# The first attention layer's values made for all head pairs at once, before the first pair

## The reference

```
parts = h @ even_w_in           # 3 query groups | keys | values, 1024 columns each | 256 cross queries
k, v  = 16 heads of 64 each
for (window, dilation) in ((128, 1), (512, 4), (2048, 16)):      # three branches, each with its own queries
    scores = q_branch . k * 64**-0.5 + relative bias, masked     # p = exp(scores - max)
mix = (sum over branches of p @ v) / (sum over branches of row sums)    # one maximum for all three
x = x + concat(mix, cross attention) @ w_out
```

## Time and profile before

| | |
|---|---|
| profiled execution, its own time | 1534.58 us |
| its span, first to last instruction | 1532.8 us |
| around the span | 1.8 us |
| TensorE busy | 1513.6 us (99%), 8132 matmuls |
| VectorE, ScalarE, GpSimd busy | 1316.3 us (86%), 1124.7 us (73%), 95.3 us (6%) |
| mean granted TensorE clock | 0.996 of 2.4 GHz |
| first layer's attention, pair 0's first projection to the end of pair 7's mix | 37.96 to 200.90 us |

### The profile page before, as it was taken

The page is one execution under the profiler, slowest core; times in us unless marked ns, Lnnn a source line. Parts: engine busy times, 40 slices in busy tenths (PEclk is TensorE's granted clock), DMA queues, the critical chain, the costliest instruction groups (busy, mean ns, idle before and its releaser), DMA issues.

```text
span 1532.8 us, 25011 instructions
## 1 busy us (share of the span) xinstructions
PE 1513.6 (99%) x8132; PEld 1280.9 (84%) x8132; DVE 1316.3 (86%) x1783; ACT 1124.7 (73%) x1487; POOL 95.3 (6%) x70
## 2 busy tenths in 40 slices
PE   9999999999999999999999999999999999999997
PEld 8999978888898788888888888888888888888886
DVE  5788868777778879998998998998998998998997
ACT  6565566544557668788788888788788888878875
POOL 2422100000030000000000000000000000000000
PEclk9999999999999989999999999999999999999999
DMA  9944546666633579999999999999999999999992
GB/s 283 241 138 137 152 129 190 190 186 192 170 90 90 164 291 369 391 380 390 381 369 389 378 374 385 380 377 376 382 396 360 384 395 358 387 391 352 401 385 112
DMA packets 225973, 455.39 MB, mean 297 GB/s; under 512 B 12848, under 2 KB 119488, under 8 KB 225920
## 3 DMA queue, kind: packets, MB, share of 16 engines
q1 hardware_dynamic: 221712, 439.52, 79.5%
q0 software_dynamic: 4208, 15.22, 3.9%
HBM read 445.52 MB, written 9.18 MB: 297 GB/s over the span
## 4 chain that ended last, share of the span: by engine, by line
PE 93%; DVE 4%; ACT 1%; issue 1%; DMA 0%; SPq 0%; ACTq 0%; DVEq 0%
PE ps L815 26%; PE ps L817 26%; PE ps L816 26%; PE ps L1139 5%; PE ps L1141 3%; PE ps L1327 2%; PE ps L931 2%; PE ps L967 1%; PE ps L947 1%; DVE w_lo L1824 1%; PE ps L1269 0%; DMA big<-in_w_mem_kv 0%; DVE X L2030 0%; DVE small L1920 0%; DVE pr L2190 0%
## 5 line engine op out<-in xcount | busy, mean ns | idle before, releaser
L1824 DVE TENSOR_TENSOR w_lo<-big,w_hi 128x1024 fp32r<-128x1024 f32 (+1 forms) x830 | 977.6, 1217 | 121.4 <-ACT w_hi L1711 52.2
L1711 ACT CAST w_hi<-big 128x1024 fp32r<-128x1024 f32 x672 | 693.5, 1056 | 139.1 <-PE ps L817 135.5
L815 PE MATMUL ps<-w_hi,m_hi 128*128 128x512 f32 (+1 forms) x1008 | 392.6, 389 | 1.5 <-DVE w_lo L1824 1.3
L817 PE MATMUL ps<-w_hi,m_lo 128*128 128x512 f32 (+1 forms) x1008 | 389.7, 387 | 0.0
L816 PE MATMUL ps<-w_lo,m_hi 128*128 128x512 f32 (+1 forms) x1008 | 389.6, 386 | 0.0
L815 PEld LDWEIGHTS ps<-w_hi,m_hi 128*128 128x128 f32 x1008 | 189.5, 188 | 41.5 <-issue 4.3
L817 PEld LDWEIGHTS ps<-w_hi,m_lo 128*128 128x128 f32 x1008 | 189.5, 188 | 38.2
L816 PEld LDWEIGHTS ps<-w_lo,m_hi 128*128 128x128 f32 x1008 | 189.6, 188 | 36.9
L1364 ACT CAST w_hi<-big 128x1024 fp32r<-128x1024 f32 (+2 forms) x166 | 164.8, 1003 | 39.5 <-PE ps L817 32.4
L815 PE MATMUL ps<-w_hi,h_two 128*128 128x512 f32 (+1 forms) x464 | 182.1, 392 | 0.0
L817 PE MATMUL ps<-w_hi,h_two 128*128 128x512 f32 (+1 forms) x464 | 179.5, 387 | 0.0
(11 more groups left out here) (309 smaller groups left out, 1560.6 us busy)
## 6 DMA issues: line engine op xcount, KB each, us to landing
big<-in_odd_w_gate SPq DMA_DIRECT2D x112, 1024.0 KB, 7.3
big<-in_odd_w_up SPq DMA_DIRECT2D x112, 1024.0 KB, 7.7
big<-in_odd_w_down SPq DMA_DIRECT2D x112, 1024.0 KB, 7.6
big<-in_even_w_in SPq DMA_DIRECT2D x42, 512.0 KB, 4.3
big<-in_even_w_gate SPq DMA_DIRECT2D x22, 512.0 KB, 4.6
big<-in_even_w_up SPq DMA_DIRECT2D x22, 512.0 KB, 3.9
big<-in_even_w_down SPq DMA_DIRECT2D x22, 512.0 KB, 4.7
big<-in_w_out SPq DMA_DIRECT2D x20, 512.0 KB, 3.7
```

Of the source, the lines that this page charges most:

```text
L815: mm(dst, a[0], b[0], start=start, stop=False, **kw)
L817: return mm(dst, a[1], b[0], start=False, stop=stop, **kw)
L1711: nc.scalar.copy(w_hi[:, slot, :], ring[s][:, (u % 2) * UNIT:(u % 2 + 1) * UNIT]).then_inc(s_hi, 1)
L1824: return V.tensor_tensor(dst, src, lead.bitcast(F32), ALU.subtract)
```

## The change

The values of all eight pairs are made before pair 0, as 256 tokens x 1024 channels with tokens as rows. The activations are the stationary side and a weight unit of one contraction chunk and 1024 columns the moving side: 12 matmuls of 512 columns for each of eight units (`values_unit`). The results lie in banks 3, 4, 2 and 7, are copied to `XH` by four copies (`values_out`), and `mix` reads them there. A step has four projections instead of five, no transposes of values and no copies of them. The slots change: eight values units stand in the list after the memory's, in slots 2, 3, 4, 5, 0, 1, 2, 3, and the pairs use slots 0 to 3. The orders of TensorE, ScalarE and VectorE in a step are changed, TensorE's steps 0 to 3 are written out too, and the wait of a pair's first projection for `third_read` moves to its second.

```
@@ Units
+        for c in range(DC):
+            add(("values", c), (c + 2) % SLOTS)
         for g in range(PAIRS):
-            for m in range(NBR + 2):
+            for m in range(NBR + 1):
                 add(("pair", 0, g, m), m)
@@ banks of the values
-        def value_bank(pair):
-            return ps[:, 5 if pair.l == 0 else 2, 0:SEQ]
+        def value_bank(t, hf):
+            return ps[:, ((3, 4), (2, 7))[t][hf], :]
@@ SyncE, stream_loads
+                for c in range(DC):
+                    load(0, 0, [U.at[("values", c)]], w_in[0][:, c:c + 1, (NBR + 1) * D:(NBR + 2) * D])
@@ TensorE, project
-                if m == 0 and norm is None:
-                    pe.wait_ge(S["third_read"], PAIRS if pair.cross else pair.g)
+                if pair.cross:
+                    pe.wait_ge(S["third_read"], PAIRS)
+                elif m == 1 and pair.g > 0:
+                    pe.wait_ge(S["third_read"], pair.g)
@@ TensorE: turn_values goes, values_unit comes
+            def values_unit(c):
+                w = split(0, 0, [U.at[("values", c)]], 1)
+                pe.wait_ge(s_nlo, DC * NORM_MIX0 + c + 1)
                 for t in range(TT):
-                    last = tr(value_bank(pair)[:, tok(t)], vT[:, tok(t)], ident)
-                last.then_inc(S["turned_v"], 1)
+                    if c == 0:
+                        pe.wait_ge(s_me, 2 * t + 2)
+                    for hf in range(2):
+                        last = mm3(value_bank(t, hf), part(HS, A_, c, tok(t)), part(w, A_, 0, slice(hf * 512, (hf + 1) * 512)),
+                                   c == 0, c == DC - 1, skip_group_check=True)
+                        if c == DC - 1 and (t, hf) != (1, 1):
+                            last.then_inc(s_vmade, 1)
+                last.then_inc(s_used, 1)
@@ TensorE, mix
-                    v = vN[:, :, :]
+                    v = XH[:, :, pair.g * P:(pair.g + 1) * P]
@@ TensorE, step and stream
-                p(0)
-                turn_values(now)
-                p(1)
+                p(0, 1, 2)
                 turn_probs(now, 0)
-                p(2, 3)
+                p(3)
                 turn_probs(now, 1)
                 scores(nxt)
-                p(4)
                 mix(now)
+                for c in range(DC):
+                    values_unit(c)
                 for m in range(first.mats):
-                    project(first, m, norm if m == 0 else None)
-                pe.wait_ge(s_me, 2 * 2)
+                    if m < 2:
+                        pe.wait_ge(s_vout, m + 1)
+                    project(first, m)
+                pe.wait_ge(s_vout, 2 * TT)
                 scores(first)
-                steps(pe, step)
+                for g in range(NPAIR):
+                    step(pair_at(0, g), *(pair_at(0, h) if h < NPAIR else None for h in (g + 1, g + 2)))
@@ ScalarE, step (even pairs)
                     e(0)
-                    values()
                     h(0)
+                    exps(now, 1)
                     e(1)
-                    exps(now, 1)
                     h(1)
+                    e(2)
                     probsT(now, 0)
-                    e(2)
                     h(2)
                     e(3)
                     probsT(now, 1)
                     h(3)
-                    e(4)
                     h(4)
@@ ScalarE, stream
-            for m in range(3):
-                hi_mat(pair_at(0, 0), m)
+            for c in range(2):
+                hi(0, 0, [U.at[("values", c)]])
             mem_out(1)
             act.wait_ge(s_scrw, 16)
...
+                for c in range(2, DC):
+                    hi(0, 0, [U.at[("values", c)]])
+                for m in range(3):
                     hi_mat(a, m)
+                for t in range(TT):
+                    for hf in range(2):
+                        values_out(t, hf)
+                hi_mat(a, 3)
@@ VectorE, step (even pairs)
                     low(0)
-                    if isinstance(now.g, int) and now.g == LATE:
-                        head_probs(now, 1)
-                        low(1)
-                    else:
-                        low(1)
-                        head_probs(now, 1)
+                    head_probs(now, 1)
+                    low(1)
                     low(2)
-                    low(3)
...
                 if nxt is not None and not now.cross:
                     head_scores(nxt)
                 if now.kind == "even":
+                    low(3)
                     low(4)
```

More of the change, by code:

```diff
@@ L250, in __init__ @@
         self.kind = "cross" if self.cross else ("even", "odd")[l]
-        self.mats = 1 if self.cross else self.nbr + 2
+        self.mats = 1 if self.cross else (NBR + 1, 3)[l]
         self.gs = gs
@@ L261, in before @@
     def before(self):
-        full = (NBR + 2, 3)[self.l]
+        full = (NBR + 1, 3)[self.l]
         return self.value(lambda g: full * g if g <= PAIRS else full * PAIRS + g - PAIRS)
     def bank(self, m):
-        full = (NBR + 2, 3)[self.l]
+        full = (NBR + 1, 3)[self.l]
         g = self.gs[0]
@@ L354, in build @@
         vT = sb("vT", [P, SEQ])
-        vN = sb("vN", [P, TT, P])
         kx = sb("kx", [P, 2 * XPAIRS, SEQ])
@@ L448, in build @@
         s_hi, s_lo, s_used = map(sem, ("unit_hi", "unit_lo", "unit_used"))
-        names = ("evacuated", "turned_v", "values", "scores", "scores_read", "masked", "max", "exp",
+        names = ("evacuated", "scores", "scores_read", "masked", "max", "exp",
                  "added", "summed", "third_left", "third_read", "probs", "probs_turned", "probsT", "mixed", "mix_hi", "mix_lo", "dve_rden")
@@ L452, in build @@
         s_me = sem("mem_evacuated")
+        s_vmade, s_vout = sem("first_values_made"), sem("first_values_out")
         s_plo = sem("unit_lo_by_pool")
@@ L759, in _ @@
             mask_pair(0, 0, True)
-            u = U.at[("pair", 0, 1, NBR + 1)]
+            u = U.at[("pair", 0, 1, NBR)]
             mask_pair(1, 1, True)
@@ L863, in product, with project @@
                 last.then_inc(s_used, 1)
-            def project(pair, m, norm=None):
+            def project(pair, m):
                 S = s_at[pair.l]
@@ L869, in project @@
                     pe.wait_ge(S["evacuated"], n - 1)
-                if m == 0 and norm is None:
-                    pe.wait_ge(S["third_read"], PAIRS if pair.cross else pair.g)
+                if pair.cross:
+                    pe.wait_ge(S["third_read"], PAIRS)
+                elif m == 1 and pair.g > 0:
+                    pe.wait_ge(S["third_read"], pair.g)
                 w = split(pair.idx, pair.span[0], pair.unit(m), DC, width(pair, m))
-                product(ps[:, pair.bank(m), 0:SEQ], w, HS, DC, norm)
+                product(ps[:, pair.bank(m), 0:SEQ], w, HS, DC)
             def project_odd(key):
@@ L942, in turn_probs @@
                 pe.wait_ge(S["probsT"], 2 * pair.g + 1 + (hh if one_bank(pair) else 0))
-                if pair.kind == "even" and not hh:
-                    pe.wait_ge(S["values"], pair.g + 1)
                 for a, b in ([(0, 0), (1, 2), (2, 1), (3, 3)] if pair.cross else [(0, 0), (1, 1), (2, 2)]):
@@ L1000, in p @@
                             project(nxt, m)
-                if isinstance(now.g, int) and now.g >= LATE:
+                if now.g >= LATE:
                     ahead = {LATE: ((), (0,)), LATE + 1: ((1, 2), (3,)), LATE + 2: ((4, 5), (6,))}[now.g]
@@ L1020, in step, with stream @@
                     return
-                p(0)
-                turn_values(now)
-                p(1)
+                p(0, 1, 2)
                 turn_probs(now, 0)
-                p(2, 3)
+                p(3)
                 turn_probs(now, 1)
                 scores(nxt)
-                p(4)
                 mix(now)
-            def stream(norm):
+            def stream():
                 pe.sem_inc(s_at[0]["mixed"], 1)
@@ L1113, in _ @@
                     norm_turn(NORM_MIX0, range(4 * (n - 3), 4 * (n - 3) + 4))
-            pe.wait_ge(s_me, 2)
-            stream(NORM_MIX0)
+            stream()
             norm_turn(NORM_FFN0)
@@ L1419, in evac @@
                     act.wait_ge(S["mixed"], 2 * pair.g - 1)
-                if not pair.cross and m == pair.nbr + 1 and not (isinstance(pair.g, int) and pair.g < 1):
-                    act.wait_ge(S["turned_v"], pair.g)
-                dst = qT[:, pair.par, m, :] if m < pair.nbr else kT[:, pair.par, :] if m == pair.nbr else vT[:, :]
+                dst = qT[:, pair.par, m, :] if m < pair.nbr else kT[:, pair.par, :]
                 nc.scalar.copy(dst, ps[:, pair.bank(m), 0:SEQ]).then_inc(S["evacuated"], 1)
@@ L1473, in e @@
                         evac((nxt, aft)[m], 0)
[L1474 to L1477, removed]
                 exps(now, 0)
@@ L1544, in step_odd, with values_out, stream @@
                     mix_hi(g)
-            def stream(done):
+            def values_out(t, hf):
+                if (t, hf) != (1, 1):
```

(20 more changed lines are left out.)

5 lines of the change are left out of this document (1 added, 4 removed).

## The result

The changed kernel takes 1539.52 us (median of 7 executions, 1538.26 to 1544.34) against 1532.77 us for the kernel before (7 executions, 1531.19 to 1534.48). The ratio is 1.0045, with a 95% interval of 1.0033 to 1.0057: 6.9 us slower, inside the range that was given (1531.5 to 1542.5), and above both the 1537.6 forecast and the 0.3% line. The direction was right; the amount, 3.0 us, was less than half of what came.

A forecast was written before the change was run, and what follows sets the result against it. TensorE was taken as the bound (93% of the chain). Later scores of pair 7 2.6, step 7 0.25 and loop hand-overs 0.2 gave 3.0 us on 1534.58: 1537.6 us, 8-in-10 range 1531.5 to 1542.5, forecast's own range 1535.0 to 1541.0.

The forecast's parts named there:

- 0.3% line: Whole kernel: differences beyond 0.3% (4.6 us) count as real; the line lies at 1539.2 us.
- What bounds, and where the change acts: TensorE bounds; only pair 0's first projection to pair 7's mix changes (162.9 us before), with differences there carried to the end.
- The values ahead: Before pair 0: 96 matmuls at 0.228 us take 21.9 us against 23.0; pair 0's scores start 19.6 us later, at 72.1.
- The stall in each step: Before projection 3, TensorE waits 0.68 us per step for ScalarE's copy of projection 1; scores 16.18 us apart.
- Step 7: Pair 7's scores to its mix's end: S + 18.67, 0.25 us more than before, S being the scores' start.
- The bank wait does not bind: Rival, chance 0.15: exponentials are never late, TensorE's list sets the pace, 6.3 us less in all, 1531.3 us.
- Late values: Rival, chance 0.18: values units' weights land late behind slot 4, TensorE stalls 5.4 us at a 14.4 us landing; 1543.0 us.
- faster wide matmuls: Rival, chance 0.04 (0.07 with other gains): 512-column values matmuls take 0.13 us instead of 0.228, saving 9.3 us; 1528.3 us.
- The loop and the back edge: TensorE's steps written out: 0.08 us a step less at the keys' hand-over, nothing gained at the back edge.
- VectorE does not bind a step: In each step VectorE's load is 15.08 us less one split of 1.13, so it does not bind.

The follow-up runs named there:

- run on the kernel before: The kernel before, unaltered, executed again for a second profile; 1534.21 us (one execution).
- run on the order: Changed kernel with ScalarE's copy of projection 1 put ahead of the second head's exponentials; 1531.62 us, ratio to the kernel before 0.9989.
- filler: Changed kernel plus fourteen matmuls with unused results in step 7, between pair 9's projection and the first transposes; 1537.06 us, ratio to before 1.0027.
- best: Changed kernel with projection 1's copy ahead of the exponentials and one output unit's split moved from step 6 to step 7; 1531.45 us, ratio to before 0.9986.
- last kernel: Changed kernel with projection 1's copy ahead of the exponentials and both output units' splits moved from step 6 to step 7; 1529.77 us, ratio to before 0.9973.

## Why the prediction came out as it did

**What bounds, and where the change acts:** right as to the work; the stretch took 169.65 us, within the 160 to 170 given. But the prediction carried a difference at the end of pair 7's mix to the end "one for one" and named a difference behind it as a sign of being wrong, and the first pair of profiles has one, -2.9 us. It is the clock at the router (run on the kernel before); whether the fall in step 7 spares a later one there stays open.

**The values ahead:** right to 0.1 us (0.228 us a matmul, pair 0's scores at +34.0).

**The stall in each step:** the mechanism was right and is shown by the run on the order, and the size was nearly right. The walk said 0.68 and a step of 16.18 us; it was 0.75 and 16.31 (16.36 for the last two). The term that was too small is the way from the scores to the exponentials, by about 0.1 us: VectorE began at +2.31 instead of +2.26 (+2.38 in the last two), ScalarE 0.09 after the addition instead of 0.02. I had taken the first from a hand-over of the cross pairs. Over seven intervals that is the 0.9 us between +2.6 and +3.5. I had added 0.2 us for loops, so the sum is short by 0.7 here.

**Step 7:** the step that failed. "S + 18.67, 0.25 us more than before." The waits were right to 0.2 us, and I wrote that the gap "is filled with waiting", without asking what 3.3 us of idle TensorE do to its clock. The sum has no term for it; it measured 2.5 us in the profiles with and without filler (21.62 and 19.09). The other 0.4 us of step 7 are hand-overs: 0.2 before the output unit and 0.2 around the second transposes. 3.0 + 0.7 + 2.5 + 0.4 = 6.6, the 6.7 us of the two pieces to rounding; the ratio gives 6.9 us. That the result still lies in the forecast's own range, 1535.0 to 1541.0, is owed to its width and not to the working: no term of it was meant for the clock. The trace of before has the evidence that such stretches exist, in the 0.8 of the profile page's clock row near the router, and I passed it by.

**The bank wait does not bind:** refuted, it was in every step. But its price was nearly right: with the wait gone the stretch and step 7 became 5.8 and 1.0 us shorter, 6.8 against the 6.3 written. The time written for it, 1531.3, is met by the run on the order (1531.62) although the clock still fell there, so that this agreement is partly luck.

**Late values, and faster wide matmuls:** both refuted by the 96 starts without idle time, 0.228 us apart.

**The loop and the back edge:** right.

**VectorE does not bind a step:** right, but by less than I said. I gave it 13.95 us of a step; it was 15.02. The last section says why.

## What to carry to other kernels

Moving work out of a software pipeline shortens its stages, and every copy that stood safely behind something long must be checked anew against the bank or buffer that it frees: walk one step on all engines, from one common event. In the list of an engine that works in order, look whether a copy that frees a bank can stand before an instruction that waits on a chain rather than behind it. When a walk leaves a gap of some microseconds on TensorE, price the clock too: what follows the gap may run at half pace. Here 1.1 us less of gap (run on the order to best) made step 7 3.5 us shorter in the profile, and filler matmuls 2.5 us. Then look at the whole execution as well: in the medians the first was worth 0.2 us, the second 2.4.

## What the hardware showed that I had not expected

- The granted clock went to half in step 7 in all profiles with 3.3 us of idle TensorE ahead of the transposes (changed kernel twice, new order) and in one with 2.15 and 0.84 us shortly after each other; not in those with filler, with 2.17 us alone, with 1.03 us, or in the three of the kernel before's order. Each time 12 matmuls of 512 columns went 0.427 us apart, not 0.228.
- Splits of 128 x 1024 on VectorE averaged 1.49 us in the changed kernel between 100 and 180 us, against 1.23 before:
```profile
L1838 DVE TENSOR_TENSOR w_lo<-big,w_hi 128x1024 fp32r<-128x1024 f32 x20 | 29.3, 1488 | 0.0
```
  One split in each step takes 2.30 us, the others 1.22. That is the 1.1 us by which I was off above. The long one is issued while GpSimd is in the middle of a part of its mask (5.5 us a step, in three parts), and ends 1.13 us after the next part starts, which is the pace of splits in a row. The split and the next part in the changed kernel, then in the kernel before:
```profile
137.40 2.30 DVE L1838 TENSOR_TENSOR w_lo<-big,w_hi 128x1024 fp32r<-128x1024 f32 x1
138.57 2.25 POOL L761 TENSOR_TENSOR big<-big,con 128x512 f32<-128x512 f32 x1
...
127.41 1.25 DVE L1824 TENSOR_TENSOR w_lo<-big,w_hi 128x1024 fp32r<-128x1024 f32 x1 [0.96 <-ACT w_hi L1364]
127.53 2.29 POOL L756 TENSOR_TENSOR big<-big,con 128x512 f32<-128x512 f32 x1
```
  137.40 + 2.30 - 138.57 = 1.13 and 127.41 + 1.25 - 127.53 = 1.13. The old order issued the split 0.1 us before the next part started and the new one 1.2 us before. It is so in all six steps of the changed kernel, of the run on the order and of the last kernel. So the traces say that the split waits for the mask's part in flight; no run without masks was made. In the changed kernel it costs no time, since VectorE then waits 1.04 us for the scores.
